# The moving and output columns of the 256-column projections taken in the order of blocks 0, 8, 1, 9, ...

## The reference

```
proj = h @ w_in                          # 2048 x 11328: q, k, v, latents, rotary key, two gates
y_a  = dilated_window_attention(q, k, v) # 16 heads of 128, three patterns merged
cq, ckv = rms_norm(latents)              # two of 512
q_b, kv = cq @ w_uq, ckv @ w_ukv         # 16 heads
y_b  = mla_attention(q_b, kv)
mix  = (g_a * (y_a @ a_w_out) + g_b * (y_b @ mla_w_out)) @ w_out
h    = layer_norm(alpha * h + mix)
y_p  = peer(h)                           # product keys, top 16 of 16384 experts for each of 8 heads:
                                         # sum of gate * gelu(down[e] . h) * up[e]
out  = layer_norm(alpha * h + y_p)
```

## Time and profile before

| | |
|---|---|
| median of 3 runs | 2432.74 us |
| time of the profiled execution | 2433.66 us |
| its span, from first to last instruction | 2431.4 us |
| TensorE busy, matmuls | 2404.8 us, 99% |
| weight loads (PEld) busy | 2207.9 us, 91% |
| VectorE / ScalarE / GpSimd busy | 1569.1 / 1197.4 / 594.7 us |
| mean granted TensorE clock | 0.998 |
| DMA | 539.01 MB, mean 222 GB/s |

### The profile page before, as it was taken

One profiled execution on the slowest core, in us unless ns is written; L12 is line 12 of the kernel. 1 busy time (PEld: TensorE's weight loads), 2 busy tenths in 40 slices (PEclk: granted clock), 3 DMA queues, 4 the chain that ended last, 5 costly groups with the idle time before them and its releaser, 6 DMA issues.

```text
span 2431.4 us, 45146 instructions
## 1 busy us (share of the span) xinstructions
PE 2404.8 (99%) x15884; PEld 2207.9 (91%) x15884; DVE 1569.1 (65%) x2615; ACT 1197.4 (49%) x1787; POOL 594.7 (24%) x427
## 2 busy tenths in 40 slices
PE   8999999999999999999999999999999999999997
PEld 8999999999999999999999999999888888888886
DVE  5555555546666666888888887755655555555556
ACT  4444444545444444666555655454444444444444
POOL 0000000000000000477668886786000000000000
PEclk9999999999999999999999999999999999999999
DMA  7667666554445665588888998988776777677764
GB/s 270 217 217 223 220 227 210 179 190 151 157 141 172 192 197 184 192 222 220 227 288 223 255 276 288 281 225 259 241 240 230 240 242 242 232 239 242 243 233 139
DMA packets 182918, 539.01 MB, mean 222 GB/s; under 512 B 53664, under 2 KB 53664, under 8 KB 180432
## 3 DMA queue, kind: packets, MB, share of 16 engines
q1 hardware_dynamic: 124128, 449.89, 56.3%
q0 software_dynamic: 54128, 71.68, 12.0%
q10 hardware_dynamic: 4608, 16.78, 2.2%
HBM read 501.42 MB, written 35.78 MB: 221 GB/s over the span
## 4 chain that ended last, share of the span: by engine, by line
PE 98%; DVE 1%; DMA 1%; ACT 0%; issue 0%; DVEq 0%; ACTq 0%; SPq 0%
PE ps L1256 38%; PE ps L1477 28%; PE ps L1452 17%; PE ps L1453 9%; PE ps L1456 1%; PE ps L1295 1%; PE ps L1310 1%; PE ps L1455 1%; PE ps L1303 0%; PE ps L1297 0%; DMA raw<-stream 0%; PE ps L1430 0%; PE ps L1311 0%; PE ps L1290 0%; DVE u_s L1209 0%; DVE u_s L1219 0%
## 5 line engine op out<-in xcount | busy, mean ns | idle before, releaser
L756 DVE TENSOR_TENSOR w_first<-raw,w_first 128x1024 fp32r<-128x1024 f32 x425 | 521.0, 1226 | 367.0 <-ACT w_first L457 355.9
L390 POOL DMA_INDIRECT g_dram<-lists x256 | 442.7, 1729 | 97.8 <-issue 79.1
L457 ACT ACTIVATE w_first<-raw 128x1024 fp32r<-128x1024 f32 x425 | 447.8, 1054 | 4.2 <-DMA raw<-stream 3.3
L756 DVE TENSOR_TENSOR w_second<-raw,w_second 128x1024 fp32r<-128x1024 f32 x299 | 365.9, 1224 | 5.4 <-ACT w_second L457 5.0
L1452 PE MATMUL ps<-a_all,w_first 128*128 128x480 f32 x1024 | 345.8, 384 | 0.2 <-DVE w_first L756 0.2
L1256 PE MATMUL ps<-a_all,w_first 128*128 128x256 f32 x2520 | 315.0, 281 | 9.2 <-DVE w_first L756 9.2
L457 ACT ACTIVATE w_second<-raw 128x1024 fp32r<-128x1024 f32 x299 | 314.6, 1052 | 7.2 <-DMA raw<-stream 6.3
L1256 PEld LDWEIGHTS ps<-a_all,w_first 128*128 128x128 f32 x2520 | 299.2, 189 | 10.2 <-issue 9.2
L1256 PE MATMUL ps<-a_all,w_second 128*128 128x256 f32 x2520 | 303.9, 276 | 0.0
L1452 PE MATMUL ps<-a_all,w_second 128*128 128x480 f32 x896 | 302.1, 382 | 0.0
L1256 PEld LDWEIGHTS ps<-a_all,w_second 128*128 128x128 f32 x2520 | 294.4, 188 | 0.0
(11 more groups left out here) (230 smaller groups left out, 3410.2 us busy)
## 6 DMA issues: line engine op xcount, KB each, us to landing
raw<-stream SPq DMA_DIRECT2D x850, 512.0 KB
g_dram<-blank POOLq DMA_DIRECT2D x32, 512.0 KB, 6.2
a_dram<-act ACTq DMA_DIRECT2D x32, 512.0 KB
a_in<-a_dram POOLq DMA_DIRECT2D x32, 512.0 KB, 5.0
g_in<-g_dram POOLq DMA_DIRECT2D x32, 512.0 KB, 6.5
g_dram<-lists POOLq DMA_INDIRECT x256
res<-x_t SPq DMA_DIRECT2D x4, 512.0 KB, 7.0
ln_s<-ln POOLq DMA_DIRECT2D x1, 2048.0 KB, 7.4
```

The source lines that it names most:

```text
L390: pool.indirect_dma_start(out=g_cell, out_offset=bass.IndirectOffsetOnAxis(ap=lists[0:n, tt, 1, j, c:c + 1], axis=0), in_=lists[0:n, tt, 2 ...
L457: act.activation(weights(t, hf, moved)[0], raw[:, t.slot(hf), :], ACT.Copy).then_inc(hi_ready, 1)
L756: dve.tensor_tensor(low, raw[:, s, :], high.bitcast(F32), ALU.subtract).then_inc(lo_ready, 1)
```

## The change

In `three`, the output and the moving operand of a matmul are viewed as two halves of eight blocks of 16 columns and walked block by block, one from the lower half, one from the upper: 0, 8, 1, 9, and so on to 7, 15. Both views are the same, so column c of the product still lands in column c of the accumulator. What was a single run of 256 elements becomes a pattern of 8 x 2 x 16 elements on either side. A block of 16 floats is 64 bytes, and two blocks that now follow one another lie 512 bytes apart (forth) or 448 bytes apart (back). The stationary operand and its load stay as they are. The query projection with its 258 columns passes `in_turn` as false and keeps its plain rows; `up_proj` uses the default and is changed too. The expert part has code of its own and is untouched. No instruction is added, taken away or moved on any engine.

```diff
+        def turned(v, n):
+
+            return v.rearrange("p (a b c) -> p b a c", a=n, c=16)
+
...
-        def three(out, w_slot, c0, cn, act_h, act_l, first, last):
+        def three(out, w_slot, c0, cn, act_h, act_l, first, last, in_turn=True):
 
             wh, wl = w_hi[w_slot][:, c0:c0 + cn], w_lo[w_slot][:, c0:c0 + cn]
             for q, (w, a) in enumerate(((wh, act_h), (wh, act_l), (wl, act_h))):
-                ins = pe.matmul(out, w, a, start=first and q == 0, stop=last and q == 2)
+                o, a = (turned(out, 2), turned(a, 2)) if in_turn else (out, a)
+                ins = pe.matmul(o, w, a, start=first and q == 0, stop=last and q == 2)
             return ins
...
-                    ins = three(acc[t.par][:, 0:n], t.slot(hf), P * k, P, ah[:, kk, 0:n], al[:, kk, 0:n], kk == 0, kk == KD - 1)
+                    ins = three(acc[t.par][:, 0:n], t.slot(hf), P * k, P, ah[:, kk, 0:n], al[:, kk, 0:n], kk == 0, kk == KD - 1, n == T)
```

## The result

The changed kernel takes 2472.86 us (median of 4 runs, 2471.63 to 2475.19) against 2432.32 us for the kernel before on the same chips (4 runs). The ratio is 1.0167, with a 95% interval of 1.015 to 1.0185. The prediction of 2432 us was wrong; the time lies inside its range of 2400 to 2475 us, which had been drawn to take in most of rival B.

A forecast was written before the change was run, and what follows sets the result against it. TensorE was taken to bound the kernel; reads and writes in the new order were priced at nothing, 0 x 7344 = 0, so the forecast stayed at 2432 us, with a range of 2400 to 2475 us.

The forecast's parts named there:

- rival B: Projections: the new order locks load and moving stream into meeting in every block, 24 or 49 us slower, 2457 or 2482; chance 0.29.
- TensorE is the bound, and what a changed matmul costs goes to the end times 7344: Whole run: TensorE is busy 99% of the span, so any change per matmul counts for all 7344 changed matmuls.
- No instruction, wait or other engine moves: All queues: instructions, waits, weight loads and their order stay as before, and neither VectorE nor ScalarE comes to bind.
- The cost of a longer description at nothing: Changed matmuls: describing an operand in several steps hides beside the 107 ns stream of the matmul ahead, costing nothing.
- The write side at nothing: PSUM output of the changed matmuls: 16 runs of 64 bytes instead of one cost nothing.
- The read side at nothing: Moving operand of the changed matmuls: 16 runs of 64 bytes cost nothing; bounds 33 us saved to 738 us lost.
- It isn't the address alone: `b_lo` matmuls, 118.0 and 113.3 ns: relative timing of moving stream and weight load sets the pace, not address alone.
- the two speeds: Plain 256-column matmuls with the same operands: 118.0 ns in latent attention, 113.3 ns in the later projection.
- second price: Changed matmuls: each break costs one more 2.4 GHz period, 6.7 ns a matmul, x 7344 = 49 us, 2482 us.
- Rival A: Projections: the new order removes collisions of moving stream and weight load, saving 33 us, 2400 us; chance 0.25.
- the second speed: The slower pace of plain 256-column matmuls, 117.8 ns in latent attention against 113.6 ns elsewhere.
- Rival C: Changed matmuls: the broken output slows them to half rate, 215 ns, adding 738 us, 3171 us; chance 0.04.

The follow-up runs named there:

- e2: Kernel before, with only the projections' writes in the turned order of 16-column blocks, reads plain: 2432.31 us.
- e1: Kernel before, with only the projections' reads of the moving operand in the turned order of 16-column blocks, writes plain: 2472.87 us.
- e14: Kernel before, plain order, with every buffer from `a_all` on 64 bytes further along: 2467.33 us.
- e19: Kernel before, plain order, with all buffers, the weights' too, 64 bytes further along: 2435.41 us.
- e20: Kernel before, plain order, with buffers from `a_all` on 128 bytes further and weights at the old place: 2440.95 us.
- e8: Kernel before, projections plain, with only the 512-column expert `up` matmuls read and written in turned blocks of 16 columns: 2464.76 us.
- e10: Changed kernel, with the second matmul of each triple in the 256-column projections using 32 of its 128 stationary columns: 2472.18 us.
- e9: Kernel before, plain order, with the second matmul of each triple in the 256-column projections using 32 of its 128 stationary columns: 2427.90 us.
- e16: Kernel before, plain output, with all 256-column projections reading the first 16 columns of their moving row 16 times over: 2480.99 us.

## Why the prediction was wrong, point by point

- *TensorE is the bound, and what a changed matmul costs goes to the end times 7344.* Right: 40.6 of 41.5 us come out by it.
- *No instruction, wait or other engine moves.* Right but for 1.5 us of waits in `down`, by the busy line and the waits. `up` and the query pieces stayed within 0.02 us.
- *The cost of a longer description at nothing.* Right: blocks of 64 have a longer description and are free.
- *The write side at nothing.* Right (`e2`).
- *The read side at nothing, because "a block of the new order is exactly the stretch after which the stream already loses a period".* This is the step that failed. I took the 17 periods for 16 columns for a period lost at every 64 bytes, paid already. A stream of runs of 16 columns loses a second one, by the reads alone (`e1`): 6.4 ns a matmul instead of 0 at the quicker speed, and 2.2 ns in latent attention, where 117.8 ns became the same 120.0. The count alone could not bear that: a mean loss of 1 in 16 doesn't say that it falls at 64-byte places. The step rested on a fit and no row tested it.
- *"It isn't the address alone".* This reading of the two speeds left the place of the buffers out of the sum. `e14`, `e19` and `e20` show that place alone can change either speed.
- *Rival B.* It came true in size: its prices of 4.2 and 6.7 ns a matmul bracket the 6.4 ns measured outside latent attention, and 2472.9 us lies between its 2457 and 2482. The second price overshot mostly because it was also charged to latent attention, which paid 2.2 ns. Its named mechanism, stream and load locked together, fell with `e8` and `e10`; its second price, one more period for each block, is what the profile after shows for blocks of 16, but as a rule it fell with blocks of 64 and of 8. I gave it 0.29 where I gave the forecast 0.42.
- *Rival A.* It fell: no order of reads came under 113 ns, nor did a load of a quarter. The sentence of "TensorE: Matmul & The Clock Gate" (the Trainium skill, "Step-by-step: what each phase is for") that a load takes nothing from the running matmul agrees with `e8`, `e9` and `e10` for both rates. Whether it holds for the second speed is open: that speed went in `e9` with the shorter load, but it moves with the place of the buffers too.
- *Rival C*, half rate from a broken output: fell with `e2`.

Open: why runs end at a cost below some length between 32 and 64 columns; what takes the 17th period in plain order; what makes the second speed; and which buffer's distance matters. The account gives the prices of short runs, not the mechanism behind them. No experiment with the full product was faster than the kernel before by more than a microsecond or so; `e9`, 5 us quicker, leaves part of it out.

## What to carry to other kernels

In this kernel a float32r matmul of 256 columns took 119.0 ns where its moving operand was read in runs of 32 columns, 119.3 to 121.1 ns in runs of 16, depending a little on the jumps, and 123.3 ns in runs of 8. Runs of 64 read as well as one plain run, and a broken PSUM output of 16-float runs was free. Before giving a new access pattern no price because a loss of the same period is already there, measure that loss with another layout: here a 64-byte shift of the buffers (`e14`) shows that plain order's 113.6 ns can become 119.2 by the layout alone, so that it is no fixed toll of one period for each 64 bytes. When a kernel's buffers are laid out anew, look at the distance between starts of its matmuls, not only at their busy time.

## What the runs showed of the hardware

- Plain float32r streams ran at 17 periods of 2.4 GHz for 16 columns at best (113.3 ns for 256), runs of 16 columns in the changed order at 18 (120.0 ns for 256, 240.1 for 512), with the clock granted in full (0.998). Both rates stayed when the load beside the matmul had 32 instead of 128 columns.
- Reading the same 64 bytes over and over was no quicker than jumping (121.1 ns, `e16`).
- A shift of 64 bytes between buffers cost plain order 35.7 us of 2431.7; in the gate tiles a shift of 128 bytes, or of everything, cost 0.1 us or nothing. `e20` still took 9.4 us more in all, 5.8 of it in `up`, and `e19` 3.8 us more, most of it in head tiles.
- In latent attention the same plain matmuls took 117.8 ns in the kernel before, 114.0 with one matmul of three narrowed to 32 stationary columns, and 113.5 to 116.0 with the moving buffers 128 bytes further along.
